# Conv tiles of the attention stage at other turns: tiles 2, 3, 4 of layer 1 and tiles 3, 4 of layer 2 stand later in a hand-written order

## The reference

```python
def conformer_conv_branch(a, g, z, w_dw, b_dw, ln_g, ln_b):
    u = a * jax.nn.sigmoid(g)
    u = depthwise_conv(u, w_dw, 31 taps, causal) + b_dw
    u = jax.nn.silu(layer_norm(u, ln_g, ln_b))
    return u * jax.nn.silu(z)

for l in range(2):
    a, g, zc, q, k, v, za, qi, ki, wi = split(h @ w_in[l])
    y_conv = conformer_conv_branch(a, g, zc, ...)
    y_attn = dsa_sparse_attention(rope(q), rope(k), v, rope(qi), rope(ki), wi, topk=132) * silu(za)
    y = concat([y_conv, y_attn]) @ w_out[l]
    h = layer_norm(ALPHA * h + y, post_ln_g[l], post_ln_b[l])
```

## Time and profile before

| | us |
|---|---|
| median of 3 runs | 1048.1 |
| lowest, highest | 1047.66, 1052.39 |
| the profiled execution's own time | 1051.77 |
| its span | 1050.0 |
| attention stage of layer 1, by TensorE's records | about 186 to 330 |
| attention stage of layer 2 | about 525 to 646 |

### The profile page before, as it was taken

How to read it: one execution, slowest core, us unless ns; L and a number is a source line. 1 busy time by engine, 2 the same in 40 slices (tenths; PEclk the granted TensorE clock), 3 DMA queues, 4 the chain that set the end, 5 groups by cost and what they waited for, 6 DMA issues and landing times.

```text
span 1050.0 us, 16512 instructions
## 1 busy us (share of the span) xinstructions
PE 996.0 (95%) x6452; PEld 842.3 (80%) x6452; DVE 652.2 (62%) x1423; ACT 581.5 (55%) x944; POOL 197.6 (19%) x238
## 2 busy tenths in 40 slices
PE   6999999998999899999999899789999899999997
PEld 6998988885677899898888677678888778887885
DVE  3899999876673389899986555627522333332522
ACT  6585891657444458588265834534656565554331
POOL 0100671013111110077011312232200000000001
PEclk9999999999999999999999899989999999999999
DMA  7775884744203667487383611865778535466651
GB/s 288 179 189 163 216 183 125 182 100 121 41 1 115 167 168 180 118 195 172 115 201 81 180 35 41 234 147 150 186 182 218 120 87 133 109 145 136 165 155 81
DMA packets 23820, 152.35 MB, mean 145 GB/s; under 512 B 2864, under 2 KB 3376, under 8 KB 6848
## 3 DMA queue, kind: packets, MB, share of 16 engines
q0 software_dynamic: 9648, 68.75, 35.2%
q1 hardware_dynamic: 14096, 82.55, 21.9%
HBM read 149.20 MB, written 2.10 MB: 144 GB/s over the span
## 4 chain that ended last, share of the span: by engine, by line
PE 80%; ACT 10%; DVE 4%; DMA 3%; issue 2%; POOL 0%; POOLq 0%; SPq 0%; DVEq 0%; ACTq 0%
PE psum_B L1257 20%; PE psum_A L1257 15%; PE psum_A L1290 9%; PE psum_B L1290 9%; PE psum_A L1439 5%; PE psum_C L1332 2%; DMA w_lo<-in_weights 2%; PE psum_A L1651 2%; PE psum_B L1439 2%; ACT w_hi L632 2%; PE psum_B L1651 2%; ACT w_lo L633 2%; PE psum_B L1393 2%; ACT exps L753 1%; PE psum_D L1257 1%
## 5 line engine op out<-in xcount | busy, mean ns | idle before, releaser
L1735 DVE SCALAR_TENSOR_TENSOR conv_acc<-u,vec,conv_acc 128x528 f32<-128x528 f32 (+1 forms) x240 | 172.3, 754 | 3.2
L1061 POOL DMA_DIRECT2D w_lo<-in_weights x67 | 59.3, 886 | 588.0 <-ACT w_lo L633 561.8
L1257 PE MATMUL psum_B<-x_hi,w_hi 128*128 128x264 f32 (+3 forms) x480 | 134.8, 321 | 5.2 <-DVE mlp_lo L2189 3.6
L632 ACT ACTIVATE w_hi<-w_raw 128x2048 fp32r<-128x2048 f32 (+2 forms) x85 | 129.5, 1523 | 12.2 <-DMA w_raw<-in_weights 11.6
L1257 PE MATMUL psum_B<-x_lo,w_hi 128*128 128x264 f32 (+3 forms) x480 | 132.6, 317 | 0.0
L1257 PE MATMUL psum_B<-x_hi,w_lo 128*128 128x264 f32 (+3 forms) x480 | 132.1, 316 | 0.0
L633 ACT ACTIVATE w_lo<-w_raw 128x2048 fp32r<-128x2048 f32 (+2 forms) x85 | 128.8, 1515 | 0.0
L1257 PE MATMUL psum_A<-x_hi,w_hi 128*128 128x264 f32 (+2 forms) x528 | 125.4, 291 | 2.2 <-DVE za L1882 1.2
L1257 PE MATMUL psum_A<-x_lo,w_hi 128*128 128x264 f32 (+2 forms) x528 | 122.7, 287 | 0.0
L1257 PE MATMUL psum_A<-x_hi,w_lo 128*128 128x264 f32 (+2 forms) x528 | 122.7, 287 | 0.0
L1257 PEld LDWEIGHTS psum_A<-x_hi,w_hi 128*128 128x128 f32 x528 | 87.5, 188 | 6.4 <-issue 3.0
(11 more groups left out here) (349 smaller groups left out, 2123.3 us busy)
## 6 DMA issues: line engine op xcount, KB each, us to landing
w_raw<-in_weights SPq DMA_DIRECT2D x67, 1024.0 KB, 5.3
w_lo<-in_weights POOLq DMA_DIRECT2D x65, 1024.0 KB, 8.5
x_first<-in_x_t SPq DMA_DIRECT2D x4, 528.0 KB, 6.9
h<-in_x SPq DMA_DIRECT2D x1, 2048.0 KB, 11.0
out<-h SPq DMA_DIRECT2D x4, 512.0 KB, 2.6
post_ln_g<-in_post_ln_g SPq DMA_DIRECT2D x2, 512.0 KB, 9.5
post_ln_b<-in_post_ln_b SPq DMA_DIRECT2D x2, 512.0 KB, 10.5
w_raw<-in_weights SPq DMA_DIRECT2D x2, 288.0 KB, 5.3
```

The lines of the kernel that those rows point to most:

```text
L632: act.activation(whi[n % RING][:, a:b], raw[n % RING][:, a:b], ACT.Copy)
L1061: pool.dma_start(wlo[n % RING][:, 0:width], io["weights"][n, :, 0:width], accum_op=ALU.add) \
L1257: mm = pe.matmul(ps[0:cols, i, 0:b - a], w[wp][:, kt, at:at + cols], x[xp][:, kt, a:b], start=(kt == 0 and wp + xp == 0), stop=(kt == KD - ...
L1735: got = dve.scalar_tensor_tensor(dst, src, w, dst, ALU.mult, ALU.add)
```

## The change

Only the table that places the conv tiles is changed. Each entry is (tile, turn of the forward transpose, bank of the forward, bank of the back transpose). All nine steps of a tile move with its turn.

```diff
 CONV_AT = {
-    0: ((0, 8, "D", "C"), (1, 10, "B", "C"), (2, 12, "D", "C"), (3, 14, "B", "C"), (4, 16, "D", "C")),
-    1: ((1, 8, "D", "C"), (2, 10, "B", "C"), (3, 12, "D", "C"), (4, 14, "B", "C")),
+    0: ((0, 8, "D", "C"), (1, 10, "B", "C"), (2, 14, "D", "C"), (3, 18, "D", "C"), (4, 22, "D", "C")),
+    1: ((1, 8, "D", "C"), (2, 10, "B", "C"), (3, 14, "D", "C"), (4, 18, "D", "C")),
 }
```

## The result

| | before | after |
|---|---|---|
| median, us | 1047.88 (4 runs) | 1060.47 (4 runs) |
| lowest, highest | 1045.80, 1052.39 | 1058.35, 1063.89 |
| the profiled execution's own time | 1051.77 | 1063.89 |
| its span | 1050.0 | 1062.1 |

The ratio is 1.0108, with a 95% interval of 1.0075 to 1.0142: **slower by 1.1%**, 12.6 us between the medians and 12.1 between the spans. The forecast was 7.7 us slower, 1055.8, with a range of 1050.5 to 1061.5.

The account below looks back on a forecast made before the run. TensorE, busy 95% of the span, was taken as the bound, so only its waits could move. First layer 3.9 plus second 3.8 gave 7.7 us, put on the median 1048.1: 1055.8, range 1050.5 to 1061.5.

Parts of the forecast that it names:

- the two rivals: Slower cases: a third half-clock stretch (1.7 to 3.4 us more, chance 0.12) and colliding transfers (up to 3.6 more, 0.08).
- each place that it named: Waits between 239 and 247 us, at turn 22's meta product, turn 25 and following logits; second-layer back transpose and next logits.
- Up to turn 17: nothing gained: First layer: cover of removed pieces becomes waiting for other engines; TensorE arrives at the same time, costed at nothing.
- All that is ahead is spent at the meta product: First layer, turn 22: TensorE, 1.07 us ahead, loses it all waiting for a weight low part; gain none.
- the collision: Rival: post-norm gain loads meet the low-part load at about 265 us, up to 3.6 us more, 1059.4; chance 0.08.
- Turns 22 to 25: 3.48: First layer: the residual of turn 22, and so the logits of turn 28, come 3.48 us late.
- the chain I named: First layer: tile 3's tanh and y, then tile 4's statistics, stand ahead of turn 22's residual, delaying turn 28's logits.
- keep both stretches and count nothing: Clock: the half-clock stretches at 240 to 246 and 587.5 to 594.5 us stay as before, adding nothing.
- a third, the rival that I gave 0.12: Another half-clock stretch from the waits of turns 22 to 25: 1.7 to 3.4 us more, 1058.3; chance 0.12.
- Second layer: 3.8: Second layer 3.8 us slower: -0.2 + 0.44 + 2.3 + 1.9 - 0.6.
- The two bank waits: Second layer, bank C: tile 4's back transpose waits 1.6 us for turn 24's logits; turn 26's logits wait 1.7 for ScalarE's affine.
- The other side: Rival: removed pieces caused the waits at turns 15 to 17, so those vanish and the clock stays up; 1041.1, chance 0.07.

Follow-up runs that it names:

- run 2: Only the second layer's row of the table changed, against the kernel before: ratio 1.0032 to the kernel before, 3.4 us.
- run 10: The kernel before, with SyncE's seven small loads of the second layer waiting for the output product of turn 17: ratio 1.0011 to the kernel before.
- run 5: The changed kernel, with y, high and low part of tile 3 in the first layer moved to turn 24: ratio 1.0068 to the kernel before.
- run 11: The changed kernel with first-layer tile 3's y, high and low part one turn later and second-layer tile 4's back transpose in bank B: 1.0040 to the kernel before.
- run 3: The changed kernel, with the first layer's post-norm gain loads waiting for the meta product's second half: ratio 1.0099 to the kernel before.
- run 4: The changed kernel, with first-layer tile 3's tanh right behind its affine and y and high part at turn 22's end: ratio 1.0070 to the kernel before.
- run 1: Only the first layer's row of the table changed, against the kernel before: ratio 1.0067 to the kernel before, 7.0 us.
- run 6: The changed kernel, with the second layer's back transpose of tile 4 in bank B instead of C: ratio 1.0081 to the kernel before.
- run 8: The kernel before, with high and low parts of conv tiles 1 to 4 one turn later: ratio 1.0024 to the kernel before.
- run 7: The kernel before, with first-layer conv tiles at turns 8, 9, 12, 16, 20 and single steps later in both layers: ratio 0.9989 to the kernel before.
- run 9: The reordered kernel of run 7, with SyncE's seven small second-layer loads waiting for the output product of turn 17: ratio 0.9953 to the kernel before.

## Why the prediction was right, and where it was short

- **The number.** 7.7 us forecast, 12.6 measured between the medians: inside the range, but 1.0 us from its end. The sum put the meta product and the clock at nothing, and they cost nearly 2 and nearly 3 us (below). The range had room above for one of the two rivals; that both together still fell inside is partly luck.
- **Sign and places.** Right: TensorE waits at each place that it named, and nowhere else of weight in the attention stages, but for the 1.84 in turn 16 of the second layer, in whose place a 1.46 in turn 15 had stood that it hadn't read.
- **Up to turn 17: nothing gained.** Right. The waits add to 4.13 where they added to 3.87, and turns 12 to 17 take 16.48 us in both.
- **All that is ahead is spent at the meta product.** The mechanism was right, the size off. I took the low part's issue and its 8.1 us as fixed. TensorE used that half 1.9 us later against the stage's clock: the issue came at 261.5, 34.9 behind turn 12 and not 33.8, and the landing took 8.8. The 1.1 goes with the clock ahead of it: the issue came 33.4, 33.8 and 35.2 behind turn 12 at a clock of 1.00, 0.89 and 0.79 (240 to 256 us) in the three traces with the first layer of before (run 2, before, run 10), and with the change's 33.7 to 33.8 at 0.79 (runs 5 and 11) and 34.9 to 35.2 at 0.68 (the other five). At 0.79 the change issues it 1.4 sooner; at its usual 0.68 that is gone. The 0.8 of the landing has no shown cause (run 3). My price for it was 0, with the collision as a rival of 0.08, and it cost nearly 2.
- **Turns 22 to 25: 3.48.** Measured 3.56, and runs 4 and 5 show that the chain I named is the cause.
- **The clock.** Here the prediction failed most. The step was: keep both stretches and count nothing. The first one grew: 0.68 from 240 to 256 us in five of the seven traces with the change's first layer and 0.79 in two, against 0.79 to 1.00 in the three of before. What the table does to bring that about isn't shown. And the trace has a third, the rival that I gave 0.12. From the logits of turn 28 to turn 39 TensorE takes 3.58 us more. Of this 0.44 is the back transpose, and 0.36 a longer wait in turn 29 (0.68 for 0.32), so the stretch cost 2.8 us, within the 1.7 to 3.4 that I had priced. Runs 1, 3 and 6 have it too (turn 23 to 39, waits included, takes them 58.5, the changed kernel 58.4 and the one before 51.2), so it isn't chance: 3.6 us of standing in two pieces, with little between, bring it each time, and in runs 4 and 5, where the waits are away, it stays away. The Trainium skill ("TensorE: Matmul & The Clock Gate", Part 1, What's actually happening) says that activity has to release the full clock; by it I should have made this stretch the forecast, and these four traces agree. I argued against it with the 4 us of work between the waits, which was no evidence. The single wait in the meta product, 1.81 to 2.30 us, was followed by a stretch in two traces of seven, so a wait of that length alone doesn't always bring one.
- **Second layer: 3.8.** Measured 2.4 in the changed kernel, 3.6 in run 2. The two bank waits were 1.66 and 1.80 for 1.6 and 1.7. That the layer lost only 2.4 comes from what lies before them: turn 12 to 18 takes 28.1 us and not 29.5. Most of this is not the change. The code of before took 28.4 there in runs 1 and 10, and 27.6 to 28.2 in the seven traces with the change, so 0.2 to 0.8 is gained where I had 0.2, and the profiled execution of before was slow by 1 us. Against runs 1 and 10 (75.5 and 75.4 for the layer) the changed kernel loses 3.5, close to the forecast. The difference between 2.4 and 3.6 is the clock again: run 2 has 0.66 in the four microseconds from 618, the changed kernel 1.00. Such a stretch came behind the two bank waits in runs 2, 4 and 5, and not in the changed kernel and run 3.
- **The other side** needed the waits at turns 15 to 17 to be due to the pieces that leave. These have left, and 4.13 us of waits are still there. Run 11, with all new waits mended but the one in the meta product, is still 0.4% slower.

## What to carry to other kernels

An instruction that is moved beside a long product takes its followers along, and in an engine that works in order they stand behind the next thing that waits for that product; look for where the last of the chain runs, not the first. Ask of every moved piece which bank or buffer it holds and who stands next in line for it (runs 6 and 8). And price the clock: here a wait of 2.2 us next to one of 1.4 cost nearly as much again behind it, so that mending the two was worth 6.0 us and not 3.6 (run 4). When order is mended, look at the weight stream next: run 7 gained nothing until loads that nobody needed yet were moved out of the way of one that was (run 9).

## What was not expected of the hardware

- The same first layer ran from 240 to 256 us with a clock of 0.89 in one execution and 1.00 in another (above), and from turn 12 to 18 took 24.98, 24.29 and 26.30 us in the traces of before, run 2 and run 10. A single trace can be 2 us off in such a place.
- The low part of a 1 MB block landed after anything from 7.8 to 13.6 us. The one issued about 12 us behind turn 12 of the second layer took 13.0 to 13.6 beside the seven small loads (before, runs 1, 7 and 8), and 10.4 to 11.3 without them (the other ten).
